# A first stage with seven x buffers, two units cut in quarters and later parameter pieces (gated conformer / S5 block, 8 cores)

## The reference, cut to what matters

```python
h = concatenate([meta, x], axis=1)              # 16 meta tokens, then 2048 frames of 2048
xn = h * rsqrt(mean(h*h, -1) + 1e-6) * norm_g   # RMSNorm
proj = einsum("bld,de->ble", xn, w_in)
v_c, g_c, z_c, u_s, z_s, gl_c, gl_s = split(proj)
y_c = conformer_conv(v_c, g_c, z_c)             # convolution, LayerNorm, swish, gate
y_s = s5_scan(u_s, ...)                         # diagonal state space, from u_s alone
y_s = gelu(y_s); y_s *= sigmoid(y_s @ w_glu + b_glu); y_s *= silu(z_s)
merged = sigmoid(gl_c + b) * (y_c @ w_conv) + sigmoid(gl_s + b) * (y_s @ w_ssm)
out = rmsnorm(h + merged @ w_out, final_g)[:, 16:]
```

## Time and profile before

| | |
|---|---|
| median of 3 runs | 1647.27 us (1646.37 to 1647.99) |
| the profiled execution's own time | 1646.79 us |
| its span, slowest core | 1645.2 us (the cores: 1642.9 to 1645.2 us) |
| mean granted TensorE clock | 0.994 of full speed on the slowest core |
| PE busy | 1603.9 us, 97% of the span |
| first transposes (T0) start | 14.30 us |
| first matmul of the next stage starts | 173.99 us |

### The profile page before, as it was taken

One profiled execution on the slowest core, in us unless ns is written; L12 is line 12 of the kernel. 1 busy time (PEld: TensorE's weight loads), 2 busy tenths in 40 slices (PEclk: granted clock), 3 DMA queues, 4 the chain that ended last, 5 costly groups with the idle time before them and its releaser, 6 DMA issues.

```text
span 1645.2 us, 22819 instructions; the slowest of 8 cores (1642.9 to 1645.2 us)
## 1 busy us (share of the span) xinstructions
PE 1603.9 (97%) x8822; PEld 771.8 (47%) x8822; DVE 739.4 (45%) x1104; ACT 501.4 (30%) x734; POOL 143.7 (9%) x228
## 2 busy tenths in 40 slices
PE   5899999999999999999999999999999999999998
PEld 2444555555544444455454444444444444444444
DVE  4664699889830003657626111122222447443333
ACT  4754577777732110003212332111111000021112
POOL 1001232223300001000000000000000000000000
PEclk8999999999999999999999999999999999999999
DMA  8823254454468325114422524166651537455553
GB/s 213 230 89 52 43 102 95 87 108 92 100 130 152 64 39 86 25 30 68 77 43 35 90 52 65 26 90 90 90 77 39 156 113 216 155 169 152 153 151 119
DMA packets 91548, 163.00 MB, mean 99 GB/s; under 512 B 62049, under 2 KB 65249, under 8 KB 82273
## 3 DMA queue, kind: packets, MB, share of 16 engines
q0 software_dynamic: 13456, 58.20, 23.5%
q1 hardware_dynamic: 19618, 88.39, 16.9%
q10 hardware_dynamic: 58368, 14.95, 5.1%
HBM read 178.03 MB, written 40.89 MB: 133 GB/s over the span
## 4 chain that ended last, share of the span: by engine, by line
PE 92%; DMA 3%; ACT 2%; DVE 1%; issue 1%; ACTq 1%; POOL 0%; DVEq 0%; SPq 0%; POOLq 0%
PE ps L257 91%; DMA wu<-wu 2%; PE ps L276 1%; ACT cs L229 1%; DMA ug<-u 1%; ACT L229 0%; ACT xs L231 0%; ACTq L871 0%; DVE xs L245 0%; DMA xt<-x 0%; PE ps L260 0%; ACT tt L229 0%; ACT gst L229 0%; ACT xm L250 0%; ACT jk L231 0%
## 5 line engine op out<-in xcount | busy, mean ns | idle before, releaser
L257 PE MATMUL ps<-xm,wr 128*128 128x512 bf16 x1280 | 293.2, 379 | 3.6 <-ACT gst L229 3.6
L257 PE MATMUL ps<-wb,xm 128*128 128x512 bf16 x1024 | 222.7, 379 | 0.0
L257 PE MATMUL ps<-xm,zr 128*128 128x512 bf16 x1024 | 222.3, 379 | 0.0
L257 PE MATMUL ps<-wo,m 128*128 128x512 bf16 (+1 forms) x1040 | 221.2, 376 | 0.0
L257 PEld LDWEIGHTS ps<-xm,wr 128*128 128x128 bf16 x1280 | 120.5, 98 | 133.7 <-issue 6.4
L257 PE MATMUL ps<-xm,gr 128*128 128x512 bf16 x768 | 169.7, 379 | 0.0
L257 PEld LDWEIGHTS ps<-wo,m 128*128 128x128 bf16 x1040 | 101.8, 98 | 119.5
L257 PEld LDWEIGHTS ps<-xm,zr 128*128 128x128 bf16 x1024 | 99.9, 98 | 119.2
L257 PEld LDWEIGHTS ps<-wb,xm 128*128 128x128 bf16 x1024 | 99.6, 98 | 118.9
L257 PE MATMUL ps<-wu,xm 128*128 128x512 bf16 x512 | 121.3, 395 | 11.9 <-DMA wu<-wu 6.4
L231 ACT ACTIVATE jk<-h 128x2048 bf16<-128x2048 f32 (+2 forms) x20 | 31.4, 1569 | 324.3 <-DVE h L245 324.3
(11 more groups left out here) (179 smaller groups left out, 1715.9 us busy)
## 6 DMA issues: line engine op xcount, KB each, us to landing
xt<-x SPq DMA_DIRECT2D x16, 1024.0 KB, 8.4
x<-x SPq DMA_DIRECT2D x16, 1024.0 KB, 8.5
out<-h SPq DMA_DIRECT2D x15, 1024.0 KB, 6.2
wr<-wm POOLq DMA_DIRECT2D x20, 512.0 KB, 8.0
gscr<-gst SPq DMA_DIRECT2D x20, 512.0 KB, 8.0
gr<-gscr SPq DMA_DIRECT2D x20, 512.0 KB, 4.5
zr<-wm POOLq DMA_DIRECT2D x16, 512.0 KB, 7.0
wob<-wo POOLq DMA_DIRECT2D x8, 1024.0 KB, 12.3
```

The costliest lines, as they stand in the source:

```text
L257: return S.op("pe", lambda e: e.matmul(out_, lhsT, rhs, start=start, stop=stop), r, w, signal=signal)
```

## The change

Four more buffers for x tiles, `xe0` to `xe3`, are laid into the upper half of XM, which is filled only from x tile 8 on. A table, `XSLOT`, says which buffer an item uses. The loads of items 3, 4 and 5 stand in the setup now, each waiting for the load two before it, and the first piece of WU[1] stands there too, waiting for item 5. The other loads follow the N's by a table, `xnext`. The units A0 and A1 are cut in quarters of four matmuls. The parameter pieces start at A10 instead of A7, one more goes behind each B, and the loads of the tables bc move from A12 to A14.

```diff
         XT = [T(f"xt{i}", [128, 2048], F32, D0 + 69632 + 8192 * i) for i in range(3)]
+        XT += [T(f"xe{i}", [128, 2048], F32, XM0 + 32768 + 8192 * i) for i in range(4)]
...
+        XSLOT = (0, 1, 2, 3, 4, 5, 0, 6, 1, 2, 5, 6, 0, 1, 2, 0, 1)
...
         ev_x[2] = load_x(2, (ev_x[0],))
+        ev_x[3] = load_x(3, (ev_x[1],))
+        ev_x[4] = load_x(4, (ev_x[2],))
+        ev_x[5] = load_x(5, (ev_x[3],))
+        load_wu(1, 0, (ev_x[5],))
         dma("sp", PRM.ap, prm_d, dsrc(), w=(PRMb,))
...
+        xnext = {0: (6, 7), 1: (8,), 2: (9,), 5: (10,), 7: (11, 12), 8: (13,), 9: (14,), 12: (15,), 13: (16,)}
+
+        def more_x(i):
+            for j in xnext.get(i, ()):
+                ev_x[j] = load_x(j, (ev_x[j - 2],))
+                if j in (7, 9, 11):
+                    load_wu(1, (j - 5) // 2, (ev_x[j],))
...
         norm(0)
-        ev_x[3] = load_x(3)
         
         norm(1)
-        ev_x[4] = load_x(4)
-        order = ["T0", "N2", "T1", "N3"]
+        more_x(0)
+        more_x(1)
+        order = ["T0", "N2", "T1", "N3", "A0:0", "A0:1", "A1:0", "A1:1", "A0:2", "A1:2", "T2", "N4", "A0:3", "A1:3", "T3",
+                 "N5"]
...
-        for i in range(NSEQ):
+        for i in range(2, NSEQ):
             order += [f"A{i}"]
...
                 norm(i)
-                ev_x[i + 3] = load_x(i + 3)
-                if i + 3 == 5:
-                    load_wu(1, 0, (ev_x[5],))
-                if i + 3 in (7, 9, 11):
-                    load_wu(1, (i + 3 - 5) // 2, (ev_x[i + 3],))
+                more_x(i)
...
+            elif ":" in o:
+                c = int(o.split(":")[1])
+                uproj(i, 0, 4 * c, 4 * c + 4)
             elif o[0] == "A":
                 uproj(i, 0)
-                if i >= 7:
+                if i >= 10:
                     next(par, None)
                     next(par, None)
-                if i == 12:
+                if i == 14:
                     for q in range(4):
                         load_bc(q)
...
             else:
                 uproj(i, 1)
+                next(par, None)
```

More of the change, by code:

```diff
@@ L346, in build @@
         XT = [T(f"xt{i}", [128, 2048], F32, D0 + 69632 + 8192 * i) for i in range(3)]
+        XT += [T(f"xe{i}", [128, 2048], F32, XM0 + 32768 + 8192 * i) for i in range(4)]
         XTb = [t.buf() for t in XT]
-        XTs = [dsrc() for _ in range(3)]
+        XTs = [dsrc() for _ in range(7)]
+        XSLOT = (0, 1, 2, 3, 4, 5, 0, 6, 1, 2, 5, 6, 0, 1, 2, 0, 1)
         SMP = T("smp", [128, 16, 64], F32, D0 + 94208)
@@ L378, in load_x @@
             t = seq[i]
-            sl = i % 3
+            sl = XSLOT[i]
             if t == "m":
@@ L445, in norm @@
             n = 16 if t == "m" else 128
-            xt, xs = XT[i % 3].ap[0:n, :], XS[i % 2].ap[0:n, :]
-            bx, bs = XTb[i % 3], XSb[i % 2]
+            xt, xs = XT[XSLOT[i]].ap[0:n, :], XS[i % 2].ap[0:n, :]
+            bx, bs = XTb[XSLOT[i]], XSb[i % 2]
             q, rr = SSQ.ap[0:n, i:i + 1], RST.ap[0:n, i:i + 1]
@@ L483, in build, with uproj @@
         ub = [0]
-        def uproj(i, nb):
+        ubank = {}
+        def uproj(i, nb, k0=0, k1=16):
             t = seq[i]
-            bk = 4 + ub[0] % 4
-            ub[0] += 1
+            if k0 == 0:
+                ubank[i, nb] = 4 + ub[0] % 4
+                ub[0] += 1
+            bk = ubank[i, nb]
             if t == "m":
@@ L493, in uproj @@
                 return
-            for k in range(16):
+            for k in range(k0, k1):
                 mm(ps[bk], xmt(t, k), WU[nb].ap[:, k, :], k == 0, k == 15,
                    r=(XMB[t], WUB[nb][k // 4]), w=(PB[bk],), signal=(k == 15))
+            if k1 < 16:
+                return
             act(U.ap[:, nb * 32:(nb + 1) * 32, t // 8, t % 8, :],
@@ L897, in build @@
         for o in order:
-            i = int(o[1:])
+            i = int(o[1:].split(":")[0])
             if o[0] == "N":
                 norm(i)
-                ev_x[i + 3] = load_x(i + 3)
-                if i + 3 == 5:
-                    load_wu(1, 0, (ev_x[5],))
-                if i + 3 in (7, 9, 11):
-                    load_wu(1, (i + 3 - 5) // 2, (ev_x[i + 3],))
+                more_x(i)
             elif o[0] == "T":
                 trans(i)
+            elif ":" in o:
+                c = int(o.split(":")[1])
+                uproj(i, 0, 4 * c, 4 * c + 4)
             elif o[0] == "A":
                 uproj(i, 0)
-                if i >= 7:
+                if i >= 10:
                     next(par, None)
                     next(par, None)
-                if i == 12:
+                if i == 14:
                     for q in range(4):
```

## The result

The changed kernel takes 1657.52 us (median of 3 runs, 1657.30 to 1658.03) against 1647.27: a ratio of 1.0062, with a 95% interval from 1.0042 to 1.0082. That is 10.25 us slower; the forecast was 8.2 us slower, in a range from 1649 to 1662.

What follows compares the result with a forecast made beforehand. PE, busy 97% of the span, was taken as the bound. T0 at 46.6, 129.3 of work and 6.5 lost make 182.4 against 173.99, 8.4 us longer: 1655.5 us, range 1649 to 1662.

Steps and rivals of the forecast that it cites:

- The patterns wait for item 5: Setup on POOL: the consts() patterns queue behind the WU[1] piece waiting for item 5, so DVE and T0 start late.
- Item 5 at 37.9, T0 at 46.6: First stage: item 5 lands at 37.9 us, and PE's first transposes, T0, start at 46.6, 32.3 us later.
- The fill costs 6.5 us: First stage behind T0: PE loses 6.5 us, bounds 4 to 12, mostly while the pipeline fills.
- 129.3: First stage: PE's work from T0 to the next stage, summed from units, transposes and small products, in us.
- Behind it the program is the same list, so the end moves as much: Behind the first stage: nothing changes, so the kernel's end moves by the stage's 8.4 us.
- 1655.5 on the median's scale: Whole kernel: the forecast time in us, after 1655.2 on the scale of the profiled execution.
- The parameter pieces, nothing, included in the smaller loss: First stage: moving parameter pieces and bc later gains nothing of its own beyond the smaller loss behind T0.
- the loss of before: First stage of the kernel before: PE loses 30.4 us after T0, all ahead of 90 us.
- the 3.29 in the earlier trace: First stage of the kernel before: a 3.29 us PE wait, put down to data and DVE.
- The quarters have nothing to hide now: First stage: A0 and A1 in quarters gain nothing, since WU[0] has landed long before.
- The first rival: Setup: the patterns pass the waiting transfer, T0 stays at 14.3, time about 1634 us; chance 0.04.
- Two signs to look for: Profile after: PE's second slice lifted from eight tenths to nine, the first lowered to about two.

Runs made afterwards that it cites:

- e1: The changed kernel with the first piece of WU[1], waiting for item 5, moved from ahead of consts() to behind it: 1639.0 us, ratio 0.9942.
- e2: The changed kernel with the first piece of WU[1] in its place but waiting for item 3 instead of item 5: 1648.3 us, ratio 1.0001.
- e3: The kernel before, with only the first piece of WU[1] put into the setup ahead of the patterns, waiting for item 2: 1651.1 us, ratio 1.0035.
- e6: e1 with the parameter pieces back from A7 and the bc loads at A12, as in the kernel before: 1644.6 us, ratio 0.9985.
- e8: The kernel before with only the parameter pieces and bc loads at their later place; old buffers, no quarters: 1640.1 us, ratio 0.9955.
- e4: e1 with A0 and A1 whole, in the order of before, instead of in quarters: 1640.2 us, ratio 0.9952.
- e7: e1 without quarters and with parameter pieces in their old place, leaving the buffers and load order: 1647.4 us, ratio 1.0003, two runs.
- e9: e8 with the quarters of A0 and A1 added, still with the three old buffers and loads: 1637.0 us, ratio 0.9942.
- e1b: The same kernel as e1, run again beside other kernels: 1636.9 us, ratio 0.9939.
- e11: e1 with the load of PRM moved back behind item 2, ahead of items 3 to 5: 1636.8 us, ratio 0.9941.

## Why the prediction was right, and where it was off

- *The patterns wait for item 5* was right, and e1, e2 and e3 show it: T0 follows the landing of the item waited for by 8.5 us, whichever it is.
- *Item 5 at 37.9, T0 at 46.6*: measured 38.05 and 46.55 on the slowest core, and 36.9 to 38.1 and 45.4 to 46.6 over the cores. That the same bytes pass in the same time held: the DMA share over the first 38 us is 0.89 after and 0.90 in the earlier trace rows. The hit to 0.2 us is in part luck: with the same loads in the setup the piece is issued at 38.3 to 39.95 in e1.
- *The fill costs 6.5 us*: on the slowest core 182.87 - 46.55 - 129.3 = 7.0. A1's first quarters came at T0 + 8.74; worked out were 8.7.
- *Behind it the program is the same list, so the end moves as much* is the step that was mis-sized. The stage's end moved by 8.9 us on the slowest cores (9.4 in the mean of the cores), the time by 10.25, and PE gets to the first matmul of the tile zr, near 800 us, 10.4 us later in the mean: 1.7 us on a core come from the clock behind the wait for amt, on four cores instead of one. This term is missing from the sum, which had it at nothing. The list is the same, but the granted clock behind the same wait is not.
- *1655.5 on the median's scale* is a slip of 0.2: 1647.27 and 8.4 make 1655.7.
- *The parameter pieces, nothing, included in the smaller loss*: without the wait on POOL their place is worth 9 us of the stage (e6, e8). The sum was right because it was made afresh behind T0 and not from the loss of before; the reading of the 3.29 in the earlier trace rows as a wait for data was wrong.
- *The quarters have nothing to hide now* was argued for the changed kernel, where WU[0] had long landed, and was not tried there. Without the wait they are worth 2 to 4 us of the stage (e4, e6 against e7, e9).
- *The first rival*, at 1634, is close to what e1 gave (1636.9 and 1639.0), so its price was some 3 to 5 us too low; its condition did not come true.
- Two signs to look for were off: PE's second slice stayed at eight tenths and did not rise to nine, since T0 lies inside that slice, and the first fell to one, not to two. The last slice, too, stands at eight tenths, before and after, which the opening of the prediction passes over.

## What to carry to other kernels

A transfer that waits for something late, put into the list of an engine that also makes early constants, holds these up too: follow each queue past the moved line, to the engine that reads what stands behind it. Price a bundle by its parts: here a part worth 9 us of the stage and one worth 2 to 4 hid behind a misplaced wait that cost some 20, and the four buffers gave nothing where the transfers were already full. A new start time is best worked out forward from the event waited for, with durations from the trace, and the work behind it summed afresh.

## What the runs showed of the hardware

A transfer that waits on POOL's list holds up the index patterns behind it, which use nothing of it: they start when its issue is over, at 38.59 us instead of 4.49 (the change against the kernel before), and at 29.55 when the wait is shorter (e2).

A 156 KB load in SP's list (PRM, in rows of 1.2 KB) delayed the x load behind it by some 3 us (ACT starts on item 3 at 26.6 to 28.4 in e1b, at 30.2 to 32.0 in e11) and let the weights of the other queue land some 2 us sooner, while the share of the DMA engines was 1.01 from 5 to 35 us in both. The place of this load is the only difference between the two kernels. At the 338 GB/s of the earlier trace rows its bytes would take 0.5 us, so they alone do not make the 3; that the short rows are the reason is not shown.

After one and the same 2.3 us wait, PE ran on at 2.4 GHz on some cores and at 1.2 GHz for a while on others (16 matmuls in 3.62 or in 5.30 us): on one core of eight before, on four after, on all eight in e1b and on none in e8. What decides it on a core was not settled.
